# Smaller weight pieces and moved combines for the last four experts of a mixture-of-experts block

## The reference

```python
def expert_step(acc, xs):
    wgu, bgu, wd, bd, g = xs
    hgu = tok @ wgu + bgu                      # wgu: 1024 x 2048
    x_glu = jnp.minimum(hgu[:, 0::2], SWIGLU_LIMIT)
    x_lin = jnp.clip(hgu[:, 1::2], -SWIGLU_LIMIT, SWIGLU_LIMIT)
    act = x_glu * jax.nn.sigmoid(SWIGLU_ALPHA * x_glu) * (x_lin + 1.0)
    out = act @ wd + bd                        # wd: 1024 x 1024
    return acc + g[:, None] * out, None
```

## Time and profile before

| | us |
|---|---|
| median of 3 runs | 1027.72 |
| the runs | 1027.57 to 1029.69 |
| the profiled execution | 1027.6 |
| its span, first to last instruction | 1025.7 |
| PE busy in it | 984.5 (96%) |
| DVE, ACT busy | 232.1, 162.7 |
| read from HBM | 418.18 MB, 409 GB/s over the span |

### The profile page before, as it was taken

One profiled execution on the slowest core, in us unless ns is written; L12 is line 12 of the kernel. 1 busy time (PEld: TensorE's weight loads), 2 busy tenths in 40 slices (PEclk: granted clock), 3 DMA queues, 4 the chain that ended last, 5 costly groups with the idle time before them and its releaser, 6 DMA issues.

```text
span 1025.7 us, 11729 instructions
## 1 busy us (share of the span) xinstructions
PE 984.5 (96%) x4756; PEld 395.0 (39%) x4756; DVE 232.1 (23%) x622; ACT 162.7 (16%) x309; POOL 34.3 (3%) x55
## 2 busy tenths in 40 slices
PE   9999999999999999999999999999999999999996
PEld 7888433333333333233333333333333333323332
DVE  6966411111111111111112011111111111111122
ACT  5763311111110110001110011111111101100112
POOL 1830000000000000000000000000000000000000
PEclk9999999999999999999999899999999999999999
DMA  8998799999999999999999999999999999999995
GB/s 246 322 401 340 306 374 428 427 427 434 429 431 431 422 431 431 436 429 429 431 429 427 429 432 435 429 427 398 432 431 438 431 432 429 429 429 427 427 424 224
DMA packets 45009, 419.64 MB, mean 409 GB/s; under 512 B 6059, under 2 KB 22587, under 8 KB 25140
## 3 DMA queue, kind: packets, MB, share of 16 engines
q1 hardware_dynamic: 44244, 418.90, 97.7%
q10 hardware_dynamic: 736, 0.34, 0.1%
HBM read 418.18 MB, written 1.05 MB: 409 GB/s over the span
## 4 chain that ended last, share of the span: by engine, by line
PE 65%; DMA 31%; ACT 1%; DVE 1%; issue 1%; SPq 0%; DVEq 0%; ACTq 0%
PE bank L1336 26%; DMA dn_ring<-in_w_down 20%; PE bank L1372 17%; DMA gu_ring<-in_w_gate_up 7%; PE bank L1143 6%; DMA dn_odd<-in_w_down 4%; PE bank L1310 4%; PE bank L1261 3%; PE bank L1164 3%; PE bank L1255 2%; ACT reg L665 1%; PE bank L1355 1%; PE bank L1349 1%; PE bank L1099 0%; PE bank L1414 0%
## 5 line engine op out<-in xcount | busy, mean ns | idle before, releaser
L1336 PE MATMUL bank<-gu_ring,reg 128*64 128x512 f32 x2048 | 448.6, 595 | 6.1 <-DMA gu_ring<-in_w_gate_up 6.1
L1336 PEld LDWEIGHTS bank<-gu_ring,reg 128*64 128x64 f32 x2048 | 143.8, 137 | 306.5 <-issue 295.1
L1372 PE MATMUL bank<-dn_ring,reg 128*64 128x512 f32 x768 | 172.2, 595 | 16.5 <-DMA dn_ring<-in_w_down 11.8
L997 DVE TENSOR_SCALAR reg<-bank 128x256 f32<-128x256 f32 x64 | 24.2, 419 | 631.8 <-PE bank L1336 631.8
L1372 PEld LDWEIGHTS bank<-dn_ring,reg 128*64 128x64 f32 x768 | 54.5, 137 | 122.7 <-issue 101.2
L660 ACT ACTIVATE reg<-reg 128x512 f32<-128x512 f32 x30 | 18.9, 629 | 467.5 <-DVE reg L997 467.5
L1310 PE MATMUL bank<-reg 64*128 64x512 f32 x256 | 63.6, 615 | 1.0 <-DVE reg L1046 0.9
L1372 PE MATMUL bank<-dn_odd,reg 128*64 128x512 f32 x256 | 58.5, 598 | 4.0 <-ACT reg L665 3.8
L1143 PE MATMUL bank<-reg,gu_ring 128*128 128x272 f32 (+1 forms) x256 | 58.8, 390 | 0.8 <-DVE reg L780 0.8
L1261 PE MATMUL bank<-xh,reg 128*64 128x512 f32 x248 | 58.5, 592 | 0.0
L667 ACT ACTIVATE reg<-bank 128x512 f32<-128x512 f32 x30 | 17.9, 597 | 230.1 <-PE bank L1372 230.1
(11 more groups left out here) (223 smaller groups left out, 446.7 us busy)
## 6 DMA issues: line engine op xcount, KB each, us to landing
gu_ring<-in_w_gate_up SPq DMA_DIRECT2D x48, 4096.0 KB, 30.1
dn_ring<-in_w_down SPq DMA_DIRECT2D x40, 2048.0 KB, 23.6
gu_ring<-in_w_gate_up SPq DMA_DIRECT2D x28, 2048.0 KB, 19.6
dn_odd<-in_w_down SPq DMA_DIRECT2D x16, 2048.0 KB, 29.3
dn_ring<-in_w_down SPq DMA_DIRECT2D x15, 1024.0 KB, 13.0
gu_ring<-in_w_in SPq DMA_DIRECT2D x16, 512.0 KB, 7.4
gu_ring<-in_w_gate_up SPq DMA_DIRECT2D x8, 1024.0 KB, 8.4
dn_ring<-in_w_out SPq DMA_DIRECT2D x4, 1024.0 KB, 8.5
```

Source lines behind the costliest of these rows:

```text
L997: ins = V.tensor_scalar(half(xglu, b), glu_v[:, 0], 7.0, None, ALU.min)
L1336: ins = mm(gub[b][64 * h:64 * h + 64, :], xgT[:, j, :], gu_ring[:, s, j, 1024 * h + 512 * b:1024 * h + 512 * b + 512], start=False, stop=( ...
L1372: ins = mm(db[64 * h:64 * h + 64, :], actT[:, at:at + SLOTS], w[:, k, 512 * h:512 * h + 512], start=(k == 0), stop=(k == KD - 1))
```

## The change

Gate/up of expert 29 comes in four quarters of 2 MB (it came in two halves of 4 MB), so expert 28 and 29 are taken out of the loop and written out. The head of down 30 comes in two pieces of two blocks, the head of down 31 in three pieces of one, one and two blocks; `down` waits for each piece at its block (`split`). A `down` can now run a hook behind a block. The combine of 29 moves from behind the gather in expert 30 to behind block j = 5 of gate_up 30. The turn of the activation of 31 moves from behind down 30 to behind block k = 5 of down 30. The combine of 30 and the turn of the gates of 31 move from ahead of down 31 to behind its block k = 3. ACT's and DVE's programs stay as they are.

```diff
+        def head_part(odd, a, b):
+            return (dn_odd if odd else dn_ring)[:, a:b, :].rearrange("p k n -> p (k n)")
+        def head_rows(e, a, b):
+            return dn_v[e, 0, :, D * a:D * b]
...
-            with sp.Fori(TURN + 1, NE // 2 - 1) as g:
+            with sp.Fori(TURN + 1, NE // 2 - 2) as g:
...
+            gu_load(1, NE - 4, NE // 2 - 3)
+            head(NE - 4, 0, NE - 6)
+            tail(NE - 4, NE - 5)
+            gu_quarters(0, NE - 3, (NE - 1, NE - 1, NE, NE))
+            head(NE - 3, 1, NE - 5)
+            tail(NE - 3, NE - 4)
             gu_quarters(1, NE - 2, (NE + 1, NE + 1, NE + 2, NE + 2))
             gu_quarters(0, NE - 1, (NE + 1, NE + 1, NE + 2, NE + 2))
-            head(NE - 2, 0, NE - 4)
+            sp.wait_ge(dn_used, (NE - 4) * 2 + 1)
+            sp.dma_start(head_part(0, 0, 2), head_rows(NE - 2, 0, 2)).then_inc(row_in[0], 16)
+            sp.dma_start(head_part(0, 2, 4), head_rows(NE - 2, 2, 4)).then_inc(head_in[0], 16)
             tail_quarters(NE - 2, NE - 3)
-            head(NE - 1, 1, NE - 3)
+            sp.wait_ge(dn_used, (NE - 3) * 2 + 1)
+            sp.dma_start(head_part(1, 0, 1), head_rows(NE - 1, 0, 1)).then_inc(row_in[1], 16)
+            sp.dma_start(head_part(1, 1, 2), head_rows(NE - 1, 1, 2)).then_inc(row_in[2], 16)
+            sp.dma_start(head_part(1, 2, 4), head_rows(NE - 1, 2, 4)).then_inc(head_in[1], 16)
...
+                    if split:
+                        if k in split:
+                            pe.wait_ge(split[k], 32 if split[k] in row_in else heads * 16)
+                    elif k == 0:
                         pe.wait_ge(head_in[odd], heads * 16)
...
                     if k in (3, 5):
                         ins.then_inc(dn_used, 1)
+                    if k in hooks:
+                        hooks[k]()
...
-                if before is not None:
+                if before is not None and not combined:
                     combine(before)
...
-            expert_up(NE - 2, 1, 4, NE - 3)
-            gate_up(NE - 1, 0, 4, NE - 2)
-            down(NE - 2, 0, NE // 2, FINE + 1, quarters=True)
-            act_turned(NE - 1)
-            combine(NE - 2)
-            pe.wait_ge(oh_ok, 2 * NE)
-            gates_turned(NE - 1)
+            def combine_29():
+                combine(NE - 3)
+            def turn_31():
+                act_turned(NE - 1)
+            def combine_30():
+                combine(NE - 2)
+                pe.wait_ge(oh_ok, 2 * NE)
+                gates_turned(NE - 1)
+            expert(NE - 4, 1, NE // 2 - 4, NE - 5, NE // 2 - 1, NE - 3 - FINE, halves=True)
+            expert(NE - 3, 0, 4, NE - 4, NE // 2 - 1, NE - 2 - FINE)
+            expert_up(NE - 2, 1, 4, NE - 3, hooks={5: combine_29}, combined=True)
+            gate_up(NE - 1, 0, 5, NE - 2)
+            down(NE - 2, 0, NE // 2, FINE + 1, quarters=True, split={0: row_in[0], 2: head_in[0]}, hooks={5: turn_31})
             pe.wait_ge(y_ok, NE - 1)
-            down(NE - 1, 1, NE // 2, FINE + 2, quarters=True, last=True)
+            down(NE - 1, 1, NE // 2, FINE + 2, quarters=True, last=True,
+                 split={0: row_in[1], 1: row_in[2], 2: head_in[1]}, hooks={3: combine_30})
```

More of the change, by code:

```diff
@@ L1356, in act_turned, with down @@
                 ins.then_inc(aT_ps, 1)
-            def down(n, odd, heads, tails, quarters=False, last=False):
+            def down(n, odd, heads, tails, quarters=False, last=False, split=None, hooks=()):
                 pe.wait_ge(aT_ok, n + 1)
                 for k in range(KD):
-                    if k == 0:
+                    if split:
+                        if k in split:
+                            pe.wait_ge(split[k], 32 if split[k] in row_in else heads * 16)
+                    elif k == 0:
                         pe.wait_ge(head_in[odd], heads * 16)
@@ L1375, in down, with expert_up @@
                         ins.then_inc(dn_used, 1)
+                    if k in hooks:
+                        hooks[k]()
                 ins.then_inc(y_ps, 1)
-            def expert_up(n, s, loads, before, hooks=(), before_turn=None, before_down=None, **pieces):
+            def expert_up(n, s, loads, before, hooks=(), before_turn=None, before_down=None, combined=False, **pieces):
                 gate_up(n, s, loads, before, hooks, **pieces)
@@ L1459, in _ @@
             add_b_down()
-            with pe.Fori(LIST + 1, NE // 2 - 1) as g:
+            with pe.Fori(LIST + 1, NE // 2 - 2) as g:
                 two_experts(g)
-            expert_up(NE - 2, 1, 4, NE - 3)
-            gate_up(NE - 1, 0, 4, NE - 2)
-            down(NE - 2, 0, NE // 2, FINE + 1, quarters=True)
-            act_turned(NE - 1)
-            combine(NE - 2)
-            pe.wait_ge(oh_ok, 2 * NE)
-            gates_turned(NE - 1)
+            def combine_29():
[11 more added lines that the diff above has]
+            down(NE - 2, 0, NE // 2, FINE + 1, quarters=True, split={0: row_in[0], 2: head_in[0]}, hooks={5: turn_31})
             pe.wait_ge(y_ok, NE - 1)
-            down(NE - 1, 1, NE // 2, FINE + 2, quarters=True, last=True)
+            down(NE - 1, 1, NE // 2, FINE + 2, quarters=True, last=True,
+                 split={0: row_in[1], 1: row_in[2], 2: head_in[1]}, hooks={3: combine_30})
             n_x = pe.value_load(qi[0:1, XCOLS:XCOLS + 1], min_val=0, max_val=XCOLS - 1)
@@ L1475, in _ @@
                 with pe.Fori(0, n_x) as q:
-                    expert_up(q + NE, 0, q + (NE // 2 - 3), q + (NE - 1), halves=True)
+                    expert_up(q + NE, 0, q + (NE // 2 - 4), q + (NE - 1), halves=True)
                     down(q + NE, 0, q + (NE // 2 + 1), q + (NE - 2 - FINE + 1))
```

## The result

The changed kernel takes 1028.69 us in the median (1027.33 to 1032.22, 20 runs) against 1027.47 for the kernel before, measured beside it (20 runs). The ratio is 1.0014 with a 95% interval of 1.0008 to 1.0019 (an estimate from all runs; the quotient of the medians is 1.0012): slower by 1.2 us in the median, and by less than the 0.2% that the prediction took as its bound. Measured once more beside the later variants it was 1028.38 against 1027.12, ratio 1.0009 (1.0001 to 1.0018). The profiled execution took 1028.74, its span is 1026.8.

A forecast was written before the change was run, and what follows sets the result against it. It took the full DMA queue (428 GB/s) as the bound, with PE tied at 998 and 1008. Last head landing 1008.6, down 31 ending 1016.4 (+0.9 us) gave 1028.5 profiled, median 1028.6; range 1026.9 to 1029.8.

The forecast's parts named there:

- gate_up 30 at 961.9: Start of gate_up 30 on PE: 1.82 us earlier, as quarters remove the wait in the middle of gate_up 29.
- gate_up 31 at 983.2: Start of gate_up 31 on PE: only 0.6 to 0.7 us earlier, with 1.1 of the 1.82 us spent.
- The stand for DVE: PE idle behind gate_up 30, ahead of the activation's turn, no longer covered by the combine of 29: about 1.0 us.
- Down 30 ends at 1004.8 to 1005.0: End of down 30 with the turn of 31 inside: the lead gone into landings, against 1005.06 before.
- Down 31 starts 1.3 us behind it, for ACT: PE stands behind down 30 while ACT makes two copies, 0.60 us each; down 31 starts at 1006.2.
- Landing of the last two blocks at 1008.6: Rest of head 31 lands 0.37 us later, its two single blocks moving at 372 GB/s against 428.
- A wait of 0.6 us ahead of k = 2: In down 31: blocks 0 and 1 run to 1008.0, then PE waits for the landing at 1008.6.
- Combine and gates' turn, 2.3 us, on the path: Behind k = 3 of down 31: the moved work is exposed, only about 0.5 of 2.3 us over a wait.
- End of down 31 at 1016.4: End of down 31: 1016.4 against 1015.47, +0.9 us, with the 10.2 us behind it unchanged.
- The rival of the PE-bound end: Head 31 lands no later than before, so PE's line decides the end: 1028.0 (1027.9 to 1028.3), chance 0.24.
- The slow queue: All 1 MB and 512 KB pieces go at 372 GB/s, end +2.0 us: 1029.7 and above, chance 0.10.
- the hidden combine: A wait behind k = 3 of down 31 covers the 2.3 us, end 0.7 us earlier: 1027.0, chance 0.07.

The follow-up runs named there:

- spare buffer kernel: Changed kernel with actT of 31 in its own buffer, down 31 in the gathers' bank, combine of 30 behind k = 1: 1026.81 us, again 1026.50.
- 512 KB kernel: Changed kernel with gate/up of 29, 30 and 31 in pieces of 512 KB: 1031.10 us, ratio 1.0042 to the kernel before.
- combine of 30 alone: Kernel before with only the combine of 30 and the gates' turn of 31 moved behind k = 3 of down 31: 1029.65 us, ratio 1.0022.

## Why the prediction was right, step by step

- **gate_up 30 at 961.9.** Measured 961.93. Right, with its reason: no wait is left in gate_up 29.
- **gate_up 31 at 983.2.** Measured 983.89. The stand for DVE was as forecast (1.0, measured 0.88 on PE). What was missed is a wait for the third quarter of gate/up 30, expected at 968 by the byte count (it was there at 967.9 in the kernel before) and present only at 969.3, behind the gap of 914.5 to 920.5, and some 0.2 us that each break between gate_up and combine costs. The wait for the fourth quarter, which the combine was to cover, was put at 0.9 and measures 1.24 where nothing covers it. The lead was gone one step earlier than forecast.
- **Down 30 ends at 1004.8 to 1005.0.** Measured 1005.8, since it began 0.5 later, lost about 0.2 ahead of k = 4, whose half tail landed at 1001.3, and the turn inside it took 0.65 us with its breaks, not 0.45.
- **Down 31 starts 1.3 us behind it, for ACT.** Measured 1.23, shown in the timeline and, by its going, in the spare buffer kernel.
- **Landing of the last two blocks at 1008.6.** Measured 1008.8. The number came close by luck. The reason given was mis-sized (0.37, measured 0.1). The rest is no cost of pieces that a run shows: in this trace the tail of 28, issued ahead of every changed transfer, already landed at 925.2 (904.67 + 20.6), when 924.0 (904.52 + 19.5) was its time before. This later stream goes with the written-out experts 28 and 29, which the prediction left among what it did not see.
- **A wait of 0.6 us ahead of k = 2.** There was none to speak of (0.1 us): PE came 0.8 later than forecast, and so just with the data, which landed at 1008.8.
- **Combine and gates' turn, 2.3 us, on the path.** 1.92 + 0.37, with no wait behind them, where the forecast allowed that up to 0.5 us might overlap one; alone they cost 2.4 us in the median and 2.1 in the trace, less what the clock took there.
- **End of down 31 at 1016.4.** Measured 1016.66. +0.9 was forecast, +1.2 measured in the median and the trace. Two misses hid each other. PE's start of down 31 was forecast 0.8 too early, of which 0.6 fell into the wait that then was not there. The pieces were put 0.27 too dear; at 0.1 the same sum gives 1016.1 and misses by 0.5. That the forecast came within 0.3 us is in part luck.

The rival of the PE-bound end had the mechanism nearer than the forecast itself: in the changed kernel no transfer stands in the end of the chain, though the landing at 1008.8 would have held PE there, had PE come any earlier. The two limits are still tied, to 0.1 us. The number of this rival, 1028.0, was low because it took down 31 to start at 1006.2 and not 1007.0. The slow queue falls by the 512 KB kernel, the hidden combine by the row behind k = 3.

What was argued and is now shown: the new order costs time (all moves without pieces +3.0, the combine of 30 alone +2.4, both with intervals clear of 1), and with PE's old order the pieces gain nothing that can be told (+0.1). With the new order the pieces take back a part of the loss: 1.8 us by the medians (+3.0 without them, +1.2 with them), 0.8 by the traces (last combine at 1018.30 and at 1017.52). Which of the two sizes is right stays open. In these traces every us of lead ends at a landing or at a wait that had been covered.

## What to carry to other kernels

When two limits are tied at the end of a kernel, a lead gained on one of them is worth only what the other leaves; follow it landing by landing before counting on it. Work that looks misplaced between two dependent steps may be what covers another engine's latency: before it moves, name the wait that it lies over (here 0.9 us for DVE and 1.2 for ACT), and move it only over a wait that is longer. To take such a wait away, a second buffer and bank, with the combine over the wait for the head, took back 1.7 to 1.9 us of the changed kernel; what it gains over the kernel before (0.5 and 0.6) is not told from nothing. And an edit that writes out turns of a loop lengthens the program: look whether the landings ahead of the edit are where they were, before the smaller pieces are blamed for a late one.

## What the runs showed of the hardware

- TensorE, idle for 2.3 us (1005.8 to 1008.1) in one execution, came back at its lower clock level, 1.2 GHz of 2.4 (granted clock 0.50 from 1008.0 to 1011.0), and lost 1.57 us. In the changed kernel, idle for 1.23 us, it kept the full clock, and so it did in the kernel with moves and no pieces after 2.54 us of idle time ahead of 943.45 (granted clock 1.00). The length of the gap alone does not tell.
- In the changed kernel, from 500 us on, a transfer's issue takes SP 0.33 to 0.43 us with up to eight outstanding, and longer with nine or ten: each of the seven issues from 950.4 to 982.6 took 3.9 to 6.5 us with 2 MB pieces ahead of it in the queue, and with 512 KB pieces ahead most issues took about 1.1. That is near the time between two landings (4.9 and 1.2 us), but five of the seven took 4.2, and no run tests what ends the hold. It cost nothing, as SP had no other work until 1003.
- The stream of weights repeats to 0.02 us over 58.6 us in three traces of kernels with the same loop, and comes 1.1 to 1.7 us later in the nine traces of kernels with two experts written out, with the rate of the windows the same (427 and 428 GB/s) and a transfer of 16 KB of instructions beside the gap. Among those nine it scatters by 0.6 us, also between two executions of the changed kernel (59.69 and 60.29). A plan that needs a landing to a few tenths of a us cannot be made from one trace.
